# Head sums on quarters of the array, query rows ahead of cache rows, and a new opening of the last feed-forward

## The reference

```python
def rmsnorm(x, g):
    r = lax.rsqrt(jnp.mean(x * x, axis=-1, keepdims=True) + EPS)
    return (x * r) * g
def convffn(h, hist, w_gate, w_up, conv_w, conv_b, w_down):
    gconv, new_hist = causal_dwconv(h @ w_gate, hist, conv_w)
    return (jax.nn.silu(gconv + conv_b) * (h @ w_up)) @ w_down, new_hist
def project_qkv(h, w_qkv, q_norm, k_norm):
    p = (h @ w_qkv).reshape(b, t, N_GROUPS, 3, H_SLOT, HEAD_DIM)   # 3 groups, 8 heads of 64
    return rmsnorm(p[:, :, :, 0], q_norm), rmsnorm(p[:, :, :, 1], k_norm), p[:, :, :, 2]
# per group (window, dilation) of (128,1), (512,4), (2048,16): softmax of q.k * SCALE + bias over
# the dilated window, groups merged by their log-sum-exp; then @ attn_w_out, residual, rmsnorm, convffn
```

## Time and profile before

| what | us |
|---|---|
| median of 3 runs | 1317.17 (1316.02 to 1317.57) |
| the profiled execution | 1316.14 |
| its span | 1314.6 |
| TensorE busy | 1298.9 |
| VectorE busy | 715.6 |
| ScalarE busy | 508.3 |

### The profile page before, as it was taken

The page is one execution under the profiler, slowest core; times in us unless marked ns, Lnnn a source line. Parts: engine busy times, 40 slices in busy tenths (PEclk is TensorE's granted clock), DMA queues, the critical chain, the costliest instruction groups (busy, mean ns, idle before and its releaser), DMA issues.

```text
span 1314.6 us, 27647 instructions
## 1 busy us (share of the span) xinstructions
PE 1298.9 (99%) x11233; PEld 1273.7 (97%) x11233; DVE 715.6 (54%) x1133; ACT 508.3 (39%) x824; POOL 21.2 (2%) x50
## 2 busy tenths in 40 slices
PE   8999999999999999999999999998999999999999
PEld 8999999999999999999999999987999999999998
DVE  6655566555556633334464655657855566553332
ACT  5222244433334432224454554455634334432211
POOL 0000000000000000000000000000000000000000
PEclk9999999999999999999999999999999999999999
DMA  7444534564444544454563656459244444445441
GB/s 200 118 155 131 161 116 141 171 192 122 138 138 124 167 138 135 140 176 126 157 196 118 211 157 201 134 146 273 81 144 133 138 156 120 156 136 167 121 105 40
DMA packets 271088, 193.15 MB, mean 147 GB/s; under 512 B 21577, under 2 KB 267329, under 8 KB 269862
## 3 DMA queue, kind: packets, MB, share of 16 engines
q1 hardware_dynamic: 267884, 137.04, 37.3%
q0 software_dynamic: 1792, 54.43, 11.4%
q10 hardware_dynamic: 1338, 0.61, 0.2%
HBM read 184.52 MB, written 64.16 MB: 189 GB/s over the span
## 4 chain that ended last, share of the span: by engine, by line
PE 95%; DVE 3%; issue 1%; ACT 1%; DMA 0%; ACTq 0%; DVEq 0%
PE acc L1680 85%; PE acc L1708 2%; PE N L1934 2%; PE M L1669 1%; PE N L1669 1%; PE M L1893 1%; PE M L1888 1%; PE acc L1916 1%; PE acc L1988 0%; PE acc L1927 0%; DVE wl L1123 0%; PE acc L2144 0%; DVE hl L1137 0%; DMA big<-in_x_sample_dram 0%; DVE x L1595 0%
## 5 line engine op out<-in xcount | busy, mean ns | idle before, releaser
L1680 PE MATMUL acc<-hh,wh 128*128 128x260 f32 x2288 | 465.9, 285 | 1.8 <-DVE wl L1123 1.6
L1680 PE MATMUL acc<-hh,wl 128*128 128x260 f32 x2288 | 461.4, 283 | 0.0
L1680 PE MATMUL acc<-hl,wh 128*128 128x260 f32 x2288 | 460.3, 283 | 0.0
L781 ACT ACTIVATE wh<-wraw 128x1024 fp32r<-128x1024 f32 (+1 forms) x211 | 219.7, 1041 | 585.8 <-PE acc L1680 580.3
L1680 PEld LDWEIGHTS acc<-hh,wh 128*128 128x128 f32 x2288 | 353.8, 189 | 4.4 <-issue 2.5
L1680 PEld LDWEIGHTS acc<-hh,wl 128*128 128x128 f32 x2288 | 352.7, 188 | 0.0
L1680 PEld LDWEIGHTS acc<-hl,wh 128*128 128x128 f32 x2288 | 351.8, 188 | 0.0
L1123 DVE TENSOR_TENSOR wl<-wraw,wh 128x1024 fp32r<-128x1024 f32 (+1 forms) x211 | 253.0, 1199 | 160.2 <-ACT wh L781 157.7
L1680 PE MATMUL acc<-yh,wh 128*128 128x260 f32 x834 | 169.4, 284 | 1.7 <-DVE x L1595 1.1
L1680 PE MATMUL acc<-yh,wl 128*128 128x260 f32 x834 | 167.7, 282 | 0.0
L1680 PE MATMUL acc<-yl,wh 128*128 128x260 f32 x834 | 167.5, 282 | 0.0
(11 more groups left out here) (223 smaller groups left out, 1000.6 us busy)
## 6 DMA issues: line engine op xcount, KB each, us to landing
out_dram<-in_cache_kv_d_dram POOLq DMA_DIRECT2D x24, 1364.0 KB, 6.2
wraw<-in_ffn_w_gate_dram SPq DMA_DIRECT2D x44, 512.0 KB, 3.8
wraw<-in_ffn_w_up_dram SPq DMA_DIRECT2D x44, 512.0 KB, 3.9
wraw<-in_attn_w_qkv_dram SPq DMA_DIRECT2D x36, 512.0 KB, 3.9
out_dram<-in_cache_kv_d_dram POOLq DMA_DIRECT2D x8, 2044.0 KB, 8.3
wraw<-in_ffn_w_down_dram SPq DMA_DIRECT2D x32, 448.0 KB, 3.7
wraw<-in_sc_w_in_dram SPq DMA_DIRECT2D x24, 512.0 KB, 4.4
wraw<-in_ffn_w_down_dram SPq DMA_DIRECT2D x16, 512.0 KB, 4.5
```

Of the source, the lines that this page charges most:

```text
L781: nc.scalar.activation(wh[c % 2][:, 0:k], wraw[:, c % 4, 0:k], ACT.Copy).then_inc(hi_done, 1)
L1680: ins = T.matmul(acc[:, par, h2, 0:HALF], w[c % 2][:, k, :], a[:, k0 + k, h2, :], start=(first and k == 0 and n == 0), stop=(last and k == ...
```

## The change

- `head_ones` becomes a 128x64 matrix full of 1/64. `squares` writes the squares of the second half of the columns with the two heads' partitions exchanged, in three operations, and `head_sums` is four products of 64x64 parts: half h2 of the columns, head h. GpSimd sets the constant with one memset, and TensorE doesn't wait for it.
- `kv_transpose` and `keep_kv` of group 0 leave out key tiles 0 to 2, which are not output.
- SP issues `query_rows_to_dram` first and `query_rows` ahead of the second `cache_rows`.
- Around the last part product, sample_probs, unit_values and sample_values are put in together ahead of its third k-step. The orders of VectorE and ScalarE behind are changed, and the first split of the feed-forward's second chunk comes after sample_y. Three identity products instead of four.
- The last outputs go to M, N, acc[:, 1], M, N, M, N, M, five of them first; squares and sums of x are taken out of the chain of hh and hl; the chunks 2 and 3 of the last feed-forward go to M and N, and their evacuation (`opened_gates`) and splits have an order of their own. ssq is no longer cleared for norms 2 and 3.

```diff
+        def wo_bank(m):
+            return (M, N, acc[:, 1], M, N, M, N, M)[m]
+        WO_FREED = (None, None, None, 0, 1, 3, 4, 5)
@@ sample_loads, c == 0 (and the same for the last pair)
+                    query_rows_to_dram(ps)
                     if ps:
                         sp.wait_ge(samp_v, ps)
                     cache_rows(ps, 0, 0, skv[:, 0], skv_in[0])
-                    query_rows_to_dram(ps)
-                    cache_rows(ps, 1, 0, skv[:, 2], skv_in[2])
                     sp.wait_ge(rowq_out, 16 * (ps + 1))
                     query_rows(ps, 0, skv[:, 1], skv_in[1])
+                    cache_rows(ps, 1, 0, skv[:, 2], skv_in[2])
@@ ScalarE, squares
-                nc.scalar.activation(sq, qk_t[:, q % 2, :].rearrange("p (h n) -> p h n", h=2),
-                                     ACT.Square).then_inc(qsq_ready, 1)
+                t = qk_t[:, q % 2, :].rearrange("p (h n) -> p h n", h=2)
+                nc.scalar.activation(sq[:, 0], t[:, 0], ACT.Square)
+                nc.scalar.activation(sq[DH:P, 1], t[0:DH, 1], ACT.Square)
+                nc.scalar.activation(sq[0:DH, 1], t[DH:P, 1], ACT.Square).then_inc(qsq_ready, 1)
@@ ScalarE, tail
+            pt_copy(n0 + 3, N, 0)
+            sample_exp(p)
+            pt_copy(n0 + 3, N, 1)
             step(S_WO, 0, 6)
-            sample_exp(p)
-            pt_copies(n0 + 3, N)
             act.wait_ge(wo3_in, 16)
             nc.scalar.activation(wo_h, wo_raw, ACT.Copy).then_inc(wo3_hi, 1)
+            pair_y(p)
             keep_values(p)
+            sample_y(p)
             step(S_WO, 0, 7)
-            pair_y(p)
-            sample_y(p)
@@ VectorE, tail
             sample_norm(p)
+            sample_pts(p, B0)
             splits(S_WO, 0, 6)
-            sample_pts(p, B0)
-            part_residual(7)
+            unit_o(n0 + 3, B1)
             dve.wait_ge(wo3_hi, 1)
             V.tensor_tensor(wo_l, wo_raw, wo_h.bitcast(F32), ALU.subtract).then_inc(wo3_lo, 1)
-            unit_o(n0 + 3, B1)
             pair_y(p)
-            splits(S_WO, 0, 7)
+            part_residual(7)
             sample_y(p)
+            splits(S_WO, 0, 7)
             last_residual(0)
             for m in range(DK):
                 if m + 1 < DK:
                     last_residual(m + 1)
-                gained(3, m, m + 3 * DK)
+                last_low(m)
+            for m in range(DK):
+                last_sum(m)
+                if m == 3:
+                    splits(S_GU1, 0, 0)
+            splits(S_GU1, 0, 1)
             rms(3)
@@ TensorE, head_sums
                 for h2 in range(2):
-                    ins = T.matmul(N[:, h2, 0:HALF], head_ones[:], sq[:, h2, :], start=True, stop=True)
+                    for h, s in enumerate(heads):
+                        ins = T.matmul(N[s, h2, 0:HALF], head_ones[heads[h ^ h2], 0:DH], sq[heads[h ^ h2], h2, :],
+                                       start=True, stop=True)
@@ TensorE, kv_transpose
-                for t in range(4):
+                for t in range(4) if g else (3,):
                     ins = transpose(N[:, 0, t * P:(t + 1) * P], qka[:, p % 2, 2 * g + 1, t * P:(t + 1) * P])
@@ TensorE, tail and opening
-            part_products(7, {1: lambda: sample_probs(p, B0), 2: lambda: sample_values(p)})
-            unit_values(n0 + 3)
+            part_products(7, {2: last_insert})      # sample_probs, unit_values(n0 + 3), sample_values
             sample_transpose(p)
-            for _ in range(4):
+            for _ in range(3):
                 T.matmul(N[:, 0, 0:P], ident[:], ident[:], start=True, stop=True)
+            for m in range(5):
+                last_output(m)
+            gate_step(0)
+            for k in range(1, 4):
+                gate_step(k)
+                last_output(4 + k)
+            gate_step(4)
+            up_step(0)
+            gate_step(5)
+            up_step(1)
+            gate_step(6)
+            gate_step(7)
+            for k in range(2, DK):
+                up_step(k)
+            for k in range(DK):
+                if k == 3:
+                    mean_square(3)
+                ins = k_step(M, 0, k, hh, hl, k == 0, k == DK - 1)
+            for k in range(DK):
+                ins = k_step(N, 1, k, hh, hl, k == 0, k == DK - 1)
...
```

More of the change, by code:

```diff
@@ L1147, in rms @@
                 V.tensor_scalar(r[:], N[:, :, 0:HALF], EPS, None, ALU.add).then_inc(ms_ready, 1)
-                if norm == 3:
-                    splits(S_GU1, 0, 0)
-                ch.after(V.memset(ssq[:], 0.0))
+                if norm < 2:
+                    ch.after(V.memset(ssq[:], 0.0))
                 dve.wait_ge(r_ready, norm + 1)
@@ L1327, in ffn, with gate_out, gate_rows, product_out @@
                 pc = PC_L[layer]
-                def gates(it, opened):
+                def gate_out(f, src):
+                    dve.wait_ge(rows_kept, f + (v0 + 1))
+                    V.tensor_tensor(u_prompt, src[:, :, 0:HP], prompt(r), ALU.mult)
+                    V.tensor_tensor(u_new, src[:, :, HP:HALF], sample(r), ALU.mult).then_inc(u_ready, 1)
+                    dve.wait_ge(u_ready, f + (v0 + 1))
+                    dve.sem_inc(acc_free, 1)
+                def gate_rows(f):
+                    dve.wait_ge(silu_ready, f + (layer * FK + 1))
+                    V.tensor_tensor(prompt(t1), conv_prompt(sv), prompt(r), ALU.mult)
+                    ch.after(V.tensor_tensor(sample(t1), conv_rows(sv), sample(r), ALU.mult))
+                def product_out(src):
+                    ch.after(V.tensor_tensor(y32[:], src[:, :, 0:HALF], t1[:], ALU.mult))
+                    dve.sem_inc(acc_free, 1)
+                    dve.sem_inc(y_ready, 1)
+                def opened_gates():
+                    ch.begin(0, 6)
+                    for i, (gate, up) in enumerate(((acc[:, 0], acc[:, 1]), (M, N))):
+                        if i == 0:
+                            dve.wait_ge(chunk_used, gu.chunk(0, 0) + 1)
+                            gate_out(0, gate)
+                        else:
+                            splits(gu, 0, 3)
+                        taps(i + v0, i, pc + FK, pc + 2 * FK)
+                        if i == 0:
+                            splits(gu, 0, 2)
+                        gate_rows(i)
+                        dve.wait_ge(chunk_used, gu.chunk(0, 2 * i + 1) + 1)
+                        product_out(up)
+                        if i == 0:
+                            dve.wait_ge(chunk_used, gu.chunk(0, 2) + 1)
+                            gate_out(1, M)
+                        y_lo(i + v0 + YOFF[layer], i)
+                def gates(it):
                     ch.begin(it, 6)
@@ L1333, in gates @@
                         dve.wait_ge(chunk_used, gu.chunk(it, 2 * i) + 1)
[L1334 to L1340, removed]
+                        gate_out(f, acc[:, 0])
+                        splits(gu, it, 2 * i)
                         taps(f + v0, f, pc + FK, pc + 2 * FK)
[L1342 to L1344 removed]
+                        gate_rows(f)
                         dve.wait_ge(chunk_used, gu.chunk(it, 2 * i + 1) + 1)
[L1346 to L1348 removed]
+                        product_out(acc[:, 1])
                         splits(gu, it, 2 * i + 1)
@@ L1836, in ffn @@
             def ffn(layer, gu, dn, y0, norm):
[L1837 to L1840, removed]
+                if norm is not None:
+                    for c in range(4):
+                        free_acc(gu, 0, c)
+                        products(gu, 0, c, c % 2, DK, hh, hl, 0, True, True, first_chunk(norm) if c == 0 else None)
+                else:
+                    for c in range(4):
+                        free_acc(gu, 1, c, 4 if c < 2 else 2)
+                        products(gu, 1, c, c % 2, DK, hh, hl, 0, True, True)
+                with pe.Fori(1 if norm is not None else 2, FK // 2) as it:
                     for c in range(4):
```

131 lines of the change are left out of this document (87 added, 44 removed).

## The result

| | before | after |
|---|---|---|
| median | 1317.37 us (4 runs, 1316.02 to 1317.73) | 1303.13 us (4 runs, 1302.91 to 1303.25) |
| profiled execution | 1316.14 | 1303.18 |
| its span | 1314.6 | 1301.6 |

The ratio is 0.9894 (95% interval 0.9882 to 0.9905): faster, by 14.2 us between the medians and 13.0 between the profiled executions. The forecast was 1302.0, and 15.2 between the profiled executions.

What follows compares the result with a forecast made beforehand. TensorE was taken to bound the kernel, busy 1298.9 of 1314.6 us. Gains of 6.4 (head sums), 1.3 (key transposes) and 7.5 (tail and opening) sum to 15.2, giving a median of 1302.0 us, range 1297 to 1310.

Steps and rivals of the forecast that it cites:

- Head sums: 24 head sums on TensorE, as four 64x64 products on quarters, take 0.59 us plus any entry: 6.4 us gained.
- A: Head-sum quarters that write the same bank run in series: only 4.5 us gained in all, 1312.7; chance 0.13.
- B: Head-sum quarters don't run together at all: 16.3 us lost, 1333.5, slower; chance 0.06.
- D: Head-sum quarters reach their bound of 0.44 us: 1297.6; chance 0.1.
- C: Last feed-forward's opening gives only 4 us, with a late start and falling clock: 1305.5; chance 0.14.
- E: Half of ScalarE's 12.7 us of extra squares reaches TensorE and eats the quarters' gain: 1308.4; chance 0.05.
- Key transposes: In kv_transpose's group 0, three of eight transposes go in four pairs: 1.3 us gained.
- Query rows first: On SP's queue the row_q write and broadcast move earlier; TensorE has no pause there, so 0 (within 0.5 us).
- VectorE's wait of 1.96: VectorE's wait before L1496 in pair 0 goes, as the query broadcast is issued earlier; worth 0 to TensorE.
- Tail: End of attention: with new orders on VectorE and ScalarE, last outputs start at 914.5 instead of 917.86: 3.4 us gained.
- Opening: Last feed-forward, first output to end of iteration 0's four gate/up chunks: 4.1 us gained from pauses and slow clock.
- 1.1 for the clock: Behind the pause before the last outputs, the fall to half clock should go: 1.1 us, inside the opening's gain.

Runs made afterwards that it cites:

- e6: Kernel after with the head sums' output banks swapped for one column half, so each row half of the array writes one bank only: 1303.40 us.
- e5: Kernel after without the partition exchange: one square of 520 columns, head sums use two quarters of the array twice: 1313.10 us.
- e3: Kernel before with only SyncE's new order, query rows ahead of the cache rows: 1316.75 us, ratio 1.0.
- e12: Kernel after with only SyncE's old order, cache rows ahead of query rows: 1305.39 us (1304.18 to 1310.98).
- e4: Kernel before with 16 instead of 4 identity products ahead of the last outputs: 1316.51 us, ratio 0.9998.
- e1: Kernel before with head sums on quarters alone (four 64x64 products, three squares on ScalarE): 1319.55 us (1311.54 to 1322.77), ratio 1.001.
- e8: Kernel after with head sums as two full-array fp32r products, one square, and sample_y ahead of part_residual(7) on VectorE: 1293.59 us.

## Why the prediction was right, and where it wasn't

**Head sums, 6.4 forecast, 4.4 to 4.6 measured.** All quarters run together, at the 0.59 to 0.60 of the earlier trace rows. The mis-sized term is 9 x (0.98 - 0.59) + 15 x (0.88 - 0.69). The 0.98 and 0.88 of the earlier trace rows run to the second pair behind the sum, and so hold the restart of the fp32r stream, while L1888's 0.59 runs to a tiled neighbour and holds none. After, the same measure is 605.15 - 604.21 - 0.24 = 0.70 and 670.33 - 669.39 - 0.24 = 0.70, and ahead of the first stands an entry of 0.33 - 0.24 = 0.09: 9 x 0.28 + 15 x 0.09 = 3.9. The other 0.5 stands at six sums with a small group right behind them, which pay no restart of the long stream. One took 0.98 (617.25 to 618.23 before) and takes 0.60 (617.10 to 617.70 after), with its entry a gain of 0.29 and not 0.09; three took 0.87 (694.40 to 695.27) and gain 0.18 instead of 0.09; two behind tiled stretches gain 0.38 instead of 0.28. That is 0.67, of which the wait for acc at 645.61, grown from 0.24 to 0.41, takes 0.1 back. The nine behind a tiled stretch are eight by the timeline: the last (872.29) stands behind a chunk, and its 0.97 comes from the tiled group behind it.

**Rivals A, B and D** are out: 0.60 and not 1.03, 1.9 or 0.44, and e6's 0.60 shows that nothing was being paid for the shared bank. The Trainium skill's rule behind A (page "TensorEngine Tiling (Array Packing)", section Restrictions and Gotchas) does not show in these products, whose row halves write the bank on different partitions; the measurement decides for this case and says nothing of products on the same partitions. The Trainium skill's rule on weight loads (page "TensorE: Matmul & The Clock Gate", section Packing small matmuls), which asks for another row group, doesn't show either: two products of each row half, and 0.60. Giving A 0.13 was fair with the trace of before. C is out by the ledger (7.6 for tail and opening), E by e5.

**Key transposes, 1.3:** five in group 0 of the four pairs, as forecast.

**Query rows first, 0: this step failed,** though the time didn't show it. "TensorE has no pause in that section, so 0" holds alone (e3) and not in company: with quarters and the old order the kernel takes 1319.55, with both 1312.17. The sum of separate effects has no place for this. The rows for it were there: the earlier trace rows priced VectorE's wait in pair 0, but the pair that mattered was the next, with a broadcast 0.4 us ahead of a 2 MB copy on a queue that TensorE paces. I followed what the moved step waited for and not what a faster TensorE would send sooner. That the step was in the change at all was luck: priced at 0, it could as well have been left out, and the kernel would then be e12, with a median of 1305.39 and runs up to 1310.98. VectorE's wait of 1.96 in pair 0 was to go, and is 1.29 after (e3's expectation says 2.0; e3 has 1.34): the write that now stands first takes 3.66 us to issue, as the key load at the head did before (3.69).

**Tail, 3.4 forecast, 3.85 measured** (4.22 less the last head sum's 0.37). The order of VectorE's operations held (six from the split at 904.49 to sample_y at 908.21; the prediction says seven), and the last outputs began 0.45 sooner against the chunks than worked out.

**Opening, 4.1 forecast, 3.8 measured.** Of its inner split, 1.1 for the clock was wrong (e4: 0.5 at most, since VectorE's 1.89 a tile was behind it), and the cadence was the larger part: 1.28 a tile after, as worked out, and one wait of 0.30 left at 914.08. The fourth split's 0.59 went.

**The median.** 15.2 was forecast between profiled executions and 13.0 came; before's profiled execution lay 1.2 below its median and after's didn't, so the medians differ by 14.2 and the forecast of 1302.0 is 1.1 off. That is partly luck: the head sums alone were 2.0 short.

## What to carry to other kernels

Before you price a speed-up of the bounding engine, list what it paces on other queues and what it doesn't: a bulk copy released by its progress moves up against transfers that wait for another transfer's landing, and a margin of 0.4 us here decided 5 us in the profiled run and 7 in the median. A part that is worth nothing alone can be what another part's gain stands on, so test parts in pairs and look at the spread of the runs, not at the median alone. A wait of TensorE can cost more than its length where the clock falls behind it, and a slow clock less than its length where another engine is behind: take both from what comes next. And take both durations of a difference with the same neighbours and to the same point.

## What the runs showed of the hardware

- A 512 KB broadcast issued 0.08 to 1.2 us behind a copy of 1364 or 2044 KB on another queue took 9.6, 9.8 and 7.9 us (e1, e12 twice); 0.05 us behind one, 6.0 (e1); with no copy just ahead, 3.7 to 5.4. How the engines share out the packets was not looked into.
- Four 64x64 products of 260 columns in fp32, on four quarters: 0.60 us; on two quarters, twice: 1.02; the full-array pair: 0.88 to 0.98 with its restart. Entry (0.09) and restart (0.10 to 0.11) cut what quarters gain from 0.28 behind a tiled stretch to 0.09 between full-array runs.
- The same sum as two full-array products in fp32r, the form of its neighbours, takes 0.25 us between chunks and 0.35 behind a tiled stretch (e8), less than the best packing here.
- Stands of TensorE of 2.75 us (before), 3.04 (e12) and 3.97 (e1) were followed by 3 to 6 us at 0.50 to 0.52 of the clock; one of 1.84 (e12) and one of 2.75 (e1) were not. Twelve more small products in place of the stand kept it at 1.00 (e4). The slow stretch cost 0.5 us or less where VectorE was behind it, and 1.6 (e1) and 2.8 (e12) where TensorE bounded.
